# Feed-forward stages on unscaled pieces of x, with 1/rms applied when the blocks' results are taken out

## What is computed

```python
# first network, per layer l; a = (2*DEPTH)**0.25
x = layer_norm(a * x + 0.5 * swiglu(x, ffn1[l]), ln1[l])
x = layer_norm(a * x + token_mixing(x, l), ln2[l])
x = layer_norm(a * x + cross_attention(x, mem, l), ln3[l])
x = layer_norm(a * x + 0.5 * swiglu(x, ffn2[l]), ln4[l])
# second network, per layer l
x = x + 0.5 * swiglu(rmsnorm(x, ffn_norm[l, 0]), ffn[l, 0])
x = x + mixer(rmsnorm(x, mix_norm[l]))          # gated linear attention + RG-LRU, then HGRN2
x = x + 0.5 * swiglu(rmsnorm(x, ffn_norm[l, 1]), ffn[l, 1])
x = x + sigmoid(rmsnorm(x, ple_norm[l]) @ ple_gate[l]) * (p[l] @ ple_proj[l])
# last
out = rmsnorm(x, final_norm)

def swiglu(x, w1, w3, w2):      # D = 1024, D_FF = 2816
    return (silu(x @ w1) * (x @ w3)) @ w2
def rmsnorm(x, g):
    return x * rsqrt(mean(x * x) + EPS) * g
def layer_norm(x, g, b):
    return (x - mean(x)) * rsqrt(var(x) + LN_EPS) * g + b
```

## Time and profile before

| | |
|---|---|
| median of 3 runs | 3031.51 us (3030.18 to 3031.66) |
| the profiled execution | 3030.65 us, its span 3028.9 us |
| mean granted TensorE clock | 0.965 of full speed |
| busy: PE, PEld | 93%, 89% |
| busy: DVE, ACT, POOL | 46%, 46%, 73% |
| chain that ended last | POOL 59%, issue 29%, PE 9% |
| read from HBM | 448.72 MB, 148 GB/s over the span |

### The profile page before, as it was taken

The page is one execution under the profiler, slowest core; times in us unless marked ns, Lnnn a source line. Parts: engine busy times, 40 slices in busy tenths (PEclk is TensorE's granted clock), DMA queues, the critical chain, the costliest instruction groups (busy, mean ns, idle before and its releaser), DMA issues.

```text
span 3028.9 us, 59383 instructions
## 1 busy us (share of the span) xinstructions
PE 2819.6 (93%) x21913; PEld 2693.3 (89%) x21920; DVE 1395.3 (46%) x2270; ACT 1381.9 (46%) x2025; POOL 2196.5 (73%) x1680
## 2 busy tenths in 40 slices
PE   8999999978999999999979998998799899998997
PEld 8989898868998989898868998997799899888997
DVE  3344524544344344524544345347533633655335
ACT  4444455444444444445444444445444544555445
POOL 8966665745996966665746986977699699766995
PEclk9999899999999999999999999999899999999999
DMA  6544333433554544343423553543355355433552
GB/s 235 180 145 159 131 126 119 140 104 112 185 181 139 180 146 162 127 135 112 149 94 124 181 180 121 182 156 125 115 191 183 126 181 180 148 131 123 191 183 84
DMA packets 122979, 451.83 MB, mean 149 GB/s; under 512 B 13650, under 2 KB 13650, under 8 KB 122196
## 3 DMA queue, kind: packets, MB, share of 16 engines
q1 hardware_dynamic: 121104, 441.43, 43.7%
q10 hardware_dynamic: 1732, 8.39, 0.7%
HBM read 448.72 MB, written 1.05 MB: 148 GB/s over the span
## 4 chain that ended last, share of the span: by engine, by line
POOL 59%; issue 29%; PE 9%; DVE 1%; POOLq 1%; ACT 1%; DVEq 0%; ACTq 0%
POOL wl L364 30%; POOL wl L363 29%; PE R L398 2%; PE R L402 2%; PE R L401 2%; PE Y L398 1%; PE Y L402 1%; PE Y L401 1%; PE R L523 1%; POOLq L369 0%; PE R L428 0%; PE R L431 0%; PE R L434 0%; DVE W L1692 0%; DVE XL L1685 0%
## 5 line engine op out<-in xcount | busy, mean ns | idle before, releaser
L363 POOL TENSOR_TENSOR wl<-raw,wh 128x512 fp32r<-128x512 f32 x836 | 1107.0, 1324 | 812.3 <-ACT wh L999 798.1
L999 ACT ACTIVATE wh<-raw 128x1024 fp32r<-128x1024 f32 x836 | 883.4, 1058 | 822.9 <-PE R L398 496.2
L398 PE MATMUL R<-XH,wh 128*128 128x256 f32 x4216 | 1213.3, 288 | 15.2 <-DVE XL L1930 7.9
L401 PE MATMUL R<-XL,wh 128*128 128x256 f32 x4216 | 1198.4, 284 | 0.0
L402 PE MATMUL R<-XH,wl 128*128 128x256 f32 x4216 | 1197.9, 284 | 0.0
L364 POOL TENSOR_TENSOR wl<-raw,wh 128x512 fp32r<-128x512 f32 x836 | 1137.5, 1361 | 0.0
L398 PEld LDWEIGHTS R<-XH,wh 128*128 128x128 f32 x4216 | 813.3, 193 | 32.5 <-issue 14.7
L401 PEld LDWEIGHTS R<-XL,wh 128*128 128x128 f32 x4216 | 813.6, 193 | 1.7 <-issue 1.0
L402 PEld LDWEIGHTS R<-XH,wl 128*128 128x128 f32 x4216 | 813.3, 193 | 0.0
L398 PE MATMUL Y<-BH,wh 128*128 128x256 f32 x1408 | 399.3, 284 | 0.9
L401 PE MATMUL Y<-BL,wh 128*128 128x256 f32 x1408 | 398.5, 283 | 0.0
(11 more groups left out here) (359 smaller groups left out, 3209.0 us busy)
## 6 DMA issues: line engine op xcount, KB each, us to landing
raw<-in_stream SPq DMA_DIRECT2D x836, 512.0 KB, 3.3
G<-in_wcmp ACTq DMA_DIRECT2D x2, 2048.0 KB, 7.5
G<-in_mem ACTq DMA_DIRECT2D x2, 1024.0 KB, 5.9
TB<-in_table SPq DMA_DIRECT2D x1, 1312.0 KB, 12.6
X<-in_x SPq DMA_DIRECT2D x2, 512.0 KB, 5.8
out_dram<-X ACTq DMA_DIRECT2D x4, 256.0 KB, 2.2
WS<-in_mix_w ACTq DMA_DIRECT2D x2, 256.0 KB
G<-in_p ACTq DMA_DIRECT2D x2, 256.0 KB, 2.6
```

The source lines that it names most:

```text
L363: pool.tensor_tensor(wl[:, s, 0:512], raw[:, r, 0:512], wh[:, s, 0:512].bitcast(F32), ALU.subtract)
L398: i = pe.matmul(o, wh[w], hi, start=start, stop=False, skip_group_check=True)
L401: pe.matmul(o, wh[w], lo, start=False, stop=False, skip_group_check=True)
L999: act.activation(wh[:, n % SPLIT, :], raw[:, n % RAW, :], ACT.Copy).then_inc(hi_done, 1)
```

## The change

Seven of the eight stages (all but the first) no longer get the normalised x. Their `norm` is gone; in its place:

- ScalarE makes the high piece of gain·X (`piece`), squares the same tile, and VectorE makes the low piece (`piece_of_x`). For a LayerNorm (`kind == "ln"`), X is centred first (`means`, `entry_ln`). After the mixers, ScalarE's pieces stand between its last block splits (`last_splits`) and VectorE's in `add_chunks`.
- TensorE sums the squares behind the opening `together`, not ahead of it, in the upper half of a PSUM bank. Then both engines make the root (`late_root`): S3 is the root, S4 what the second half of the product needs (0.25·root² for RMSNorm, 0.25·root for LayerNorm).
- `hidden_rms` and `hidden_ln` apply it when they take a chunk out. For LayerNorm the bias of the norm is carried by two further columns in XHB and XLB: matmuls of 258 columns give the bias's product in column 256. These stages' chunk loop is written out on VectorE, and for chunks 2 to 9 `scaled` brings the eight tiles of X, which the stage's sum needs, to their normalised value.

The core of the diff:

```diff
@@ ffn, TensorE
-            def ffn(ready):
+            def ffn(kind, sums=None):
+                hi, lo, width = (XHB, XLB, T + 2) if kind == "ln" else (XH, XL, T)
...
-                together(2, XH, XL, ready)
+                if kind == "rms":
+                    sums = claim()
+                together(2, hi, lo, split_ready, width)
+                if kind != "first":
+                    for c in range(DC):
+                        from_act()
+                        i = pe.matmul(sums[:, T:2 * T], ONES, W8[:, c, :], start=c == 0, stop=c == DC - 1, skip_group_check=True)
+                    i.then_inc(chunk_ready, 1)
@@ ScalarE
+            def piece(c, gain):
+                from_dve()
+                give_dve(act.activation(XH[:, c, :], X[:, c, :], ACT.Identity, scale=gain(c)))
+                give_pe(act.activation(W8[:, c, :], X[:, c, :], ACT.Square))
...
+            def last_splits(gain):
+                for c in range(DC - 1):
+                    split_next()
+                    if c == 0:
+                        act.preload_act_table_set("natural_log_exp_and_others")
+                    for p in {1: (0,), 2: (1, 2), 3: (3,), 4: (4,), 5: (5,), 6: (6, 7)}.get(c, ()):
+                        piece(p, gain)
+                skip(DC)
+            def late_root(eps):
+                m = t.n["chunk"]
+                act.wait_ge(chunk_ready, m + 3)
+                skip(1)
+                step(act.activation(S2[:, 0:T], R[:, m % RING, T:2 * T], ACT.Ln, scale=1.0 / D, bias=EPS[:, eps:eps + 1]))
+                give_dve(act.activation(S3[:, 0:T], S2[:, 0:T], ACT.Exp, scale=-0.5))
+                act.preload_act_table_set("exp_and_others")
...
+                        from_dve()
+                        give_dve(act.activation(EB[:, j % 2, :], M[:, 2 + j % 2, :], ACT.Tanh, scale=0.5))
@@ VectorE
+            def hidden_rms(j):
+                m, o = chunk()
+                give_act(tt_(a, o[:, 0:T], S3[:, 0:T], ALU.mult))
+                from_act()
+                take(stt(e, e, 1.0, o[:, 0:T], ALU.add, ALU.mult), m)
+                m, o = chunk()
+                take(tt_(v, o[:, 0:T], S4[:, 0:T], ALU.mult), m)
+                step(tt_(h, e, v, ALU.mult))
+                split_hidden(j)
+            def hidden_ln(j):
+                m, o = chunk()
+                tt_(a, o[:, 0:T], S3[:, 0:T], ALU.mult)
+                take(dve.tensor_copy(b1, o[:, T:T + 1]), m)
+                give_act(ts_(a, a, b1, None, ALU.add))
+                from_act()
+                step(stt(e, e, 1.0, a, ALU.add, ALU.mult))
+                m, o = chunk()
+                tt_(v, o[:, 0:T], S4[:, 0:T], ALU.mult)
+                take(ts_(b3, o[:, T:T + 1], 0.25, None, ALU.mult), m)
+                step(stt(h, v, b3, e, ALU.add, ALU.mult))
+                split_hidden(j)
...
+                def scaled(c):
+                    step(stt(X[:, c, :], X[:, c, :], gain(c), S3[:, 0:T], ALU.mult, ALU.mult))
+                    step(ts_(X[:, c, :], X[:, c, :], bias(c), None, ALU.add))
...
+                if kind == "ln":
+                    for j in range(1, FC - 1):
+                        hidden(j)
+                        if 2 <= j < 2 + DC:
+                            scaled(j - 2)
...
+            def late_root(eps):
+                from_act()
+                m = t.n["chunk"]
+                skip(1)
+                v, y, w, q = S2[:, 0:T], S3[:, 0:T], S4[:, T:2 * T], S4[:, 0:T]
+                take(ts_(v, R[:, m % RING, T:2 * T], 1.0 / D, eps, ALU.mult, ALU.add), m)
+                step(tt_(w, y, y, ALU.mult))
+                step(stt(w, w, -0.5, v, ALU.mult, ALU.mult))
+                step(stt(y, w, 1.5, y, ALU.add, ALU.mult))
+                if eps == RMS_EPS:
+                    step(stt(q, y, 0.25, y, ALU.mult, ALU.mult))
+                else:
+                    step(ts_(q, y, 0.25, None, ALU.mult))
+            def entry_ln(gain, bias):
...
+                need(mean_ready)
+                for c in range(DC):
+                    give_act(stt(X[:, c, :], R[:, m % RING, 0:T], -1.0 / D, X[:, c, :], ALU.mult, ALU.add))
+                    if c > 0:
+                        piece_of_x(c - 1, gain)
+                piece_of_x(DC - 1, gain)
+                late_root(LN_EPS)
...
+            def piece_of_x(c, gain):
+                from_act()
+                give_pe(stt(XL[:, c, :], X[:, c, :], gain(c), XH[:, c, :].bitcast(F32), ALU.mult, ALU.subtract))
```

More of the change, by code:

```diff
@@ L1067, in ffn @@
                        **{("raw", r): 32 for r in range(RAW)}}
+                if kind != "first":
+                    per[dve_act] = 4
                 with act.Fori(0, (FC - 2) // 4) as it:
@@ L1357, in gla, with hgrn @@
                 piece_hi(3, flat(O[:, 2:4, :]))
-                for _ in range(DC - 1):
-                    split_next()
-                skip(DC)
-            def hgrn():
+                last_splits(after)
+            def hgrn(after):
                 base = t.n["chunk"]
@@ new lines, in ffn @@
+            def ffn(kind, late=None, gain=None, bias=None):
+                hidden = {"first": hidden_first, "rms": hidden_rms, "ln": hidden_ln}[kind]
+                def scaled(c):
+                    step(stt(X[:, c, :], X[:, c, :], gain(c), S3[:, 0:T], ALU.mult, ALU.mult))
+                    step(ts_(X[:, c, :], X[:, c, :], bias(c), None, ALU.add))
+                hidden(0)
+                if kind == "ln":
[3 more added lines that the diff above has]
+                            scaled(j - 2)
+                else:
+                    per = {"chunk": 8, dve_step: 4, dve_pe: 4, act_dve: 4, **{("round", b): 2 for b in range(RING)}}
+                    if kind == "rms":
+                        per[dve_act], per[dve_step] = 4, 8
+                    with dve.Fori(0, (FC - 2) // 4) as it:
+                        t.enter(it, per)
+                        for j in range(4):
+                            hidden(j + 1)
+                        t.leave((FC - 2) // 4)
```

173 lines of the change are left out of this document (101 added, 72 removed).

## The result

The changed kernel takes 3045.85 us (median of 5, 3043.08 to 3049.8), the kernel before beside it 3030.18 us (3028.57 to 3031.66): a ratio of 1.0054 (95% interval 1.0039 to 1.0069). It is slower, as forecast, but by 16 us and not by 37. The profiled execution took 3045.85 us.

The account below looks back on a forecast made before the run. Inside a stage TensorE was taken as the bound, with GpSimd close behind. Costs of 69.3 us less 32.3 saved at the entries gave +37.0 on 3031.5: 3068.5 us, range 3034 to 3100.

Parts of the forecast that it names:

- (e): Matmuls of 258 columns in place of 256, 1056 in each of three stages: +2.6 us.
- (c): Rescaling X in chunks 2 to 9 of LayerNorm stages: VectorE's period 10.0 us, 9.0 us of waiting per stage, +27.0.
- (f): Half clock behind three of four RMSNorm waits for the second block of pair 1, 1.7 us each: +5.0 us.
- (d): Last hidden chunk, covered by one down-projection alone: +0.4 us per RMSNorm stage, +1.8 per LayerNorm stage, +7.0 together.
- entries, LayerNorm (3): Ahead of the three LayerNorm stages, the opening no longer waits for the root: 6.2 us saved each.
- entries, RMSNorm (4): Ahead of RMSNorm stages: 4.8 us saved after each mixer, 0.7 after the first block's last LayerNorm, 3.3 after the gate stage.
- (a): Second block of pair 1, its split now behind squares, Ln, Exp and table load: 3.07 us waiting at seven entries, +21.5.
- (b): First hidden chunk, behind VectorE's root: 0.1 us of waiting in an RMSNorm stage, 2.0 in a LayerNorm one, +6.2 together.
- rival 2: VectorE's new instructions keep their short 0.42 and 0.35 us next to GpSimd: faster, 3023 us; chance 0.12.
- rival 4: The lag is worse, VectorE's period at its upper end or GpSimd itself the bound: 3107 us; chance 0.10.
- Rival 1: The rescaling of X fits into VectorE's idle time and costs nothing: sum +10, 3042 us; chance 0.16.
- Rival 3: Matmuls of 258 columns fall out of the fast pace, 0.35 us more each, 1100 us in all; chance 0.02.

Follow-up runs that it names:

- e1: The kernel before with only the rows of the two piece buffers of x lengthened from 256 to 258 numbers: 3011.06 us, ratio 0.9939.
- e4: The changed kernel with ScalarE's split of a stage's fourth weight block issued ahead of the root: 3038.62 us, ratio 1.0041 to the kernel before.
- e3: The changed kernel without the sixteen instructions that rescale X in each LayerNorm stage: 3029.27 us, ratio 1.0004 to the kernel before.
- e8: The changed kernel with LayerNorm stages as before; in RMSNorm stages, squares ahead of the opening and a product moved earlier: 2988.73 us.
- e10: The kernel before with 64 unused bytes ahead of XH, so all four piece buffers start 64 bytes behind a multiple of 1024: 2984.93 us.
- e11: The kernel before with unused buffers so that only the low pieces, XL and BL, start 128 bytes behind a multiple of 1024: 2988.87 us.
- e9: The kernel before with 128 unused bytes ahead of XH, so all four piece buffers start 128 bytes behind a multiple of 1024: 3013.64 us.

## Why the forecast was too high

Against e1, which has the changed kernel's buffers and none of its instructions, the changed kernel costs 33.0 us (15.7 above the kernel before, where e1 is 17.3 below); the forecast's sum was 37.0. What failed is the step ahead of the sum: a hidden chunk's pair as "72 matmuls of 0.12 us, 8.64 us" was carried over to the kernel after, and the edit of the buffers was priced in (e) alone, as two more columns. The longer rows moved the operands, and that gave back 17.3 us over the whole kernel. That the rest of the sum comes so close is in part luck: of its terms, (c) was 15.7 us too dear, (f) 10.7 and (d) 5.9 too cheap, as the table shows. The terms, each from the stages and entries of the changed kernel against e1 (a wait with the first matmul behind it; one execution each):

| term | forecast | measured |
|---|---|---|
| entries, LayerNorm (3) | −18.7 | −22.3 |
| entries, RMSNorm (4) | −13.6 | −14.6 |
| (a) second block of pair 1 (7) | +21.5 | +23.3 |
| (b) first hidden chunk | +6.2 | +3.2 |
| (c) rescaling | +27.0 | +11.3 |
| (d) last chunk | +7.0 | +12.9 |
| (e) 258 columns | +2.6 | +3.4 |
| (f) half clock | +5.0 | +15.7 |

The measured column sums to +32.9; the two profiled spans, 3044.1 and 3011.4, lie 32.7 apart.

*Entries: right.* At ln3 7.2 us against 6.2. Behind the two mixers 4.5 and 5.0 us against 4.8, behind the gate stage 3.4 against 3.3, behind the first block's last LayerNorm 1.7 against 0.7.

*(a) right, for its mechanism and size.* In the changed kernel ScalarE, then GpSimd, at the first LayerNorm stage:

```profile
707.50 0.47 ACT L1102 ACTIVATE S<-R,EPS 128x256 f32<-128x256 f32 x1 [4.74 <-PE R L526]
...
708.45 1.28 ACT L1104 ACT_TABLE_LOAD   x1
709.74 1.06 ACT L1018 ACTIVATE wh<-raw 128x1024 fp32r<-128x1024 f32 x1
...
710.88 1.26 POOL L366 TENSOR_TENSOR wl<-raw,wh 128x512 fp32r<-128x512 f32 x1 [19.11 <-ACT wh L1018]
712.10 1.32 POOL L367 TENSOR_TENSOR wl<-raw,wh 128x512 fp32r<-128x512 f32 x1
```

The split starts 1.29 us behind the start of the table load, as in the earlier trace rows; the drain of the Trainium skill ("ScalarE: Activation LUTs", What ACT_TABLE_LOAD costs) is not to be seen in this place either. What the prediction had not seen is that (a) hides most of a wait of its own kind. It had priced "0.1 of waiting" for an RMSNorm stage's first chunk behind (a), which was right, but this also meant that (a) could not be won back alone. e4 showed it.

*(b): right.* (The parts that the prediction gives for it, 0.1 in four stages and 2.0 in three, make 6.4, not 6.2.) In the three LayerNorm stages the low piece of the first hidden chunk ends 11.2, 11.1 and 11.1 us behind the squares, where 10.9 was forecast. In the first and second of them:

```profile
716.83 1.40 DVE L1640 TENSOR_TENSOR BL<-W,BH 128x256 fp32r<-128x256 f32 x1
...
930.86 1.39 DVE L1640 TENSOR_TENSOR BL<-W,BH 128x256 fp32r<-128x256 f32 x1
```

Yet TensorE waits 1.75 us for it in the first and 0.36 and 0.45 in the others, because there it came later itself: the clock fell behind (a), which takes from this wait what it costs. Stretches of both, from the end of (a) to the end of that piece (clock granted 1.00, then 0.68):

```profile
713.47:718.23 4.76, 3.13 (x24) 2.93 (x24) 4.62 (x6) 1.31 (x2) 4.28 (x4) 1.00 0.42 131
...
927.53:932.25 4.72, 4.48 (x24) 4.27 (x24) 4.58 (x6) 1.31 (x2) 4.28 (x4) 0.68 0.45 129
```

So some 2.7 us that the table counts under (f) stand in the place of (b); the prediction had said that (b) hides the clock there, and in these two stages it does.

*(c): too dear,* for the count of locked instructions that run at full length. The prediction took a period of 10.0 us for every rescaled chunk. The groups of VectorE in the changed kernel (busy us, mean ns) show what the two inputs or the place in the period do:

```profile
L1682 DVE SCALAR_TENSOR_TENSOR X<-X,SM,S 128x256 f32<-128x256 f32 x24 | 33.5, 1396 | 0.8
L1683 DVE TENSOR_SCALAR X<-X,SM 128x256 f32<-128x256 f32 x24 | 30.4, 1265 | 0.8
...
L1674 DVE SCALAR_TENSOR_TENSOR W<-W,BB,M 128x256 f32<-128x256 f32 x66 | 67.3, 1020 | 2.3
...
L1659 DVE TENSOR_TENSOR W<-M,W 128x256 f32<-128x256 f32 x88 | 48.1, 546 | 3.0
...
L1654 DVE TENSOR_TENSOR M<-R,S 128x256 f32<-128x256 f32 x88 | 37.4, 425 | 159.8 <-PE R L405 159.0 <-DVE BL L1640 0.7
```

The lock's two durations are as in the earlier trace rows, so rival 2 falls. The Trainium skill ("SBUF — State Buffer", SBUF: two separate sides) says the same of a VectorE instruction with two SBUF inputs beside GpSimd: whoever starts first holds the shared ports to the end of the instruction. The trace agrees. In an RMSNorm chunk the new product (L1659) takes less than 0.6 us in 74 of 88 chunks: it starts in the last 0.3 us of one half-block of GpSimd, mostly 0.1 us before its end, and so ahead of the next, which then lasts 1.51 us where the mean is 1.37. The other 14 start earlier in a half-block, take 0.6 to 1.6 us and bring the mean to 546 ns. With a period of 9.4 in place of 10.0, eight chunks lag 6.1 us; less the 2.4 that GpSimd's lead covers, 3.7 are left, which is the 3.6 to 3.9 of each stage. The lead was right; the period was the step that failed, and it takes rival 4 (11.6) with it. The waits come three to a stage and 18.8 us apart, not six and 10.

*(d): too cheap.* "GpSimd is partly idle by then" was wrong: at the end of a stage it is at work on the blocks of the next, so the product takes 1.48 us, and the chain is 4.64 us long; the 4.6 named as the most was the value. All seven stages wait some 2 us. For the three LayerNorm stages the forecast's 1.8 us over the kernel before was right; the miss is in the four RMSNorm stages, 0.4 forecast and 1.8 to 1.9 measured.

*(f): right as a mechanism, a third of its size.* The granted clock behind (a) is 0.62 in the mean over 4.5 us, a part of them at 1.2 GHz; in the earlier trace rows it was 0.50. Matmuls at half clock cost 0.3 to 3.2 us above the pace in each of the seven stages, at the last chunk as well as at the first blocks; the prediction had counted three places, none of them in a LayerNorm stage or at a last chunk.

Rival 1, the rescaling absorbed, gave 3042 and came closest to the total, but by luck: the waits for the rescaling are there. It would have needed e3 to show nothing, and e3 is 14.8 us faster. Rival 3 falls too: matmuls of 258 columns follow each other at 0.1201 us in the changed kernel, those of 256 at 0.1189, which is (e).

## What to carry to other kernels

Where TensorE is the bound, the place of its operands in SBUF is a tuning parameter of its own. A few dozen unused bytes were worth 1.4% here, more than the restructuring (0.7% in its best form, e8 against e1), and a change that resizes or adds a buffer must be compared with a kernel that has the same buffers. When a late result is waited for in two places, price the second wait as if the first were gone before you remove the first; here starting the shared chain earlier won both. When a sum of terms comes out near the total, look at each term: here three that were off by 6 to 16 us nearly cancelled. And place an instruction that is long beside GpSimd where its engine would idle anyway, ahead of the arrival that the chain hangs on.

## What the runs showed of the hardware

- A stream of fp32r matmuls of 256 columns at full granted clock runs at 0.1200, some 0.1188 or 0.1178 us each, depending on where in SBUF its moving operands start (multiples of 256 bytes against 32 to 128 bytes more), in one stage of e10 at 0.1135 and in one of e11 at 0.1167. The table of the places above has the numbers. The Trainium skill ("SBUF — State Buffer", Who interferes with whom) names one point of contention among the engines, the ports that VectorE and GpSimd share. In e1 no instruction differs from the kernel before, on any engine, and the pitch does (0.1200 and 0.1189), so the dependence seen here is another one, on the places of TensorE's own operands. Why it is there stays open: whether the weights or the result in PSUM take part, beside the other piece, was not tried.
- The pitch is not fixed by the places alone: e9, e10 and e11 each changed it between stages of one execution, with the same code and the same places.
- The loss to half clock behind a wait of 3.3 us differs widely for the same code: in the changed kernel's four RMSNorm stages some 3.2, 2.6, 2.9 and 0.4 us, that behind the last chunk's wait taken in.
- A VectorE instruction with two SBUF inputs that starts 0.1 us before one of GpSimd's ends, and so ahead of its next, keeps its short length (0.43 us against 1.40); GpSimd's next is the longer for it (1.51 us against 1.37 in the mean).
